# Making the high and low part of a weight unit in one operation each over 1024 columns, in two slots of a unit instead of four of a half

## The reference

```python
for l in range(2):                                   # first block
    q, k, v, u_pool, ga, gp = split(xn @ w_in[l])    # 1024 x 4096
    merged = sigmoid(ga) * (attn(q, k, v) @ w_attn_o[l]) + sigmoid(gp) * (pool(u_pool) @ w_pool_o[l])
    x = x + g1 * (merged @ w_out[l])
    x = x + g2 * peer_ffn(xf, w_query[l], sub_keys[l], expert_u[l], expert_v[l])  # all 16384 experts
# second block: half-step SwiGLU feed-forwards around neighbourhood attention (layer 0) or a short convolution (layer 1)
x = layer_norm(alpha * x + 0.5 * gate * (silu(a) * u) @ ffn_w_out, g, b)
```

## Time and profile before

| | |
|---|---|
| median of 3 runs | 4274.32 us (4267.85 to 4274.61) |
| profiled execution | span 4273.0 us, from the first to the last instruction of the program |
| TensorE matmul busy | 4056.4 us, 95% |
| VectorE busy | 2736.9 us, 64% |
| ScalarE busy | 1983.0 us, 46% |
| GpSimd busy | 105.5 us, 2% |
| mean granted TensorE clock | 0.974 of full speed |

### The profile page before, as it was taken

One profiled execution on the slowest core, in us unless ns is written; L12 is line 12 of the kernel. 1 busy time (PEld: TensorE's weight loads), 2 busy tenths in 40 slices (PEclk: granted clock), 3 DMA queues, 4 the chain that ended last, 5 costly groups with the idle time before them and its releaser, 6 DMA issues.

```text
span 4273.0 us, 85154 instructions
## 1 busy us (share of the span) xinstructions
PE 4056.4 (95%) x29544; PEld 3598.5 (84%) x29544; DVE 2736.9 (64%) x5356; ACT 1983.0 (46%) x3929; POOL 105.5 (2%) x131
## 2 busy tenths in 40 slices
PE   8999889999999999979999999989999989999998
PEld 1889245999999988824799999989999869898898
DVE  0564976666666665487666666666566665656665
ACT  0554066444444454317544444445454444444444
POOL 0000000000000000000000000001001010001010
PEclk9999989999999999989999999999999999999999
DMA  8334734555555434554455555575554315454454
GB/s 277 131 134 156 254 133 143 182 182 182 182 182 182 167 124 143 186 198 167 146 183 182 182 182 182 182 199 176 170 184 148 109 50 182 143 182 142 148 172 138
DMA packets 195899, 714.28 MB, mean 167 GB/s; under 512 B 21696, under 2 KB 22080, under 8 KB 195520
## 3 DMA queue, kind: packets, MB, share of 16 engines
q1 hardware_dynamic: 194112, 705.08, 49.5%
q0 software_dynamic: 1664, 7.57, 0.8%
HBM read 711.52 MB, written 1.05 MB: 167 GB/s over the span
## 4 chain that ended last, share of the span: by engine, by line
PE 56%; PEld 28%; DVE 10%; issue 3%; ACT 2%; PEldq 1%; DMA 1%; DVEq 0%; ACTq 0%; POOL 0%; SPq 0%; POOLq 0%
PE bank L1560 14%; PE bank L1562 14%; PE bank L1561 14%; PEld bank L1562 11%; PEld bank L1560 10%; PEld bank L1561 7%; PE bank L1676 6%; PE bank L1849 2%; PE bank L1657 2%; PE bank L1850 1%; DVE wl L898 1%; PE bank L1820 1%; PE bank L1966 1%; DVE arena L1009 0%; DVE arena L1258 0%
## 5 line engine op out<-in xcount | busy, mean ns | idle before, releaser
L898 DVE TENSOR_TENSOR wl<-raw,wh 128x512 fp32r<-128x512 f32 x2180 | 1508.3, 704 | 1082.8 <-ACT wh L520 1081.2
L520 ACT ACTIVATE wh<-raw 128x512 fp32r<-128x512 f32 x2180 | 1344.2, 629 | 1255.7 <-PE bank L1562 1251.7
L1560 PE MATMUL bank<-XH,wh 128*128 128x256 f32 x5184 | 1497.8, 289 | 97.2 <-DVE XL L1000 51.7
L1561 PE MATMUL bank<-XL,wh 128*128 128x256 f32 x5184 | 1480.9, 286 | 0.0
L1562 PE MATMUL bank<-XH,wl 128*128 128x256 f32 x5184 | 1480.4, 286 | 0.0
L1560 PEld LDWEIGHTS bank<-XH,wh 128*128 128x128 f32 x5184 | 1007.8, 194 | 118.9 <-issue 82.9
L1561 PEld LDWEIGHTS bank<-XL,wh 128*128 128x128 f32 x5184 | 1010.5, 195 | 1.1 <-issue 1.0
L1562 PEld LDWEIGHTS bank<-XH,wl 128*128 128x128 f32 x5184 | 1009.5, 195 | 0.0
L1560 PE MATMUL bank<-AH,wh 128*128 128x256 f32 x2928 | 828.7, 283 | 0.0
L1561 PE MATMUL bank<-AL,wh 128*128 128x256 f32 x2928 | 828.6, 283 | 0.0
L1562 PE MATMUL bank<-AH,wl 128*128 128x256 f32 x2928 | 828.6, 283 | 0.0
(11 more groups left out here) (223 smaller groups left out, 3251.7 us busy)
## 6 DMA issues: line engine op xcount, KB each, us to landing
raw<-stream SPq DMA_DIRECT2D x1340, 512.0 KB, 3.3
arena<-rpb POOLq DMA_DIRECT2D x4, 1024.0 KB, 24.5
arena<-tables POOLq DMA_DIRECT2D x2, 832.0 KB, 7.7
X<-x_t SPq DMA_DIRECT2D x1, 1024.0 KB, 7.8
arena<-ctx_t POOLq DMA_DIRECT2D x1, 1024.0 KB, 8.7
out_t<-X SPq DMA_DIRECT2D x4, 256.0 KB, 2.1
arena<-tables POOLq DMA_DIRECT2D x1, 608.0 KB, 14.4
cols<-columns SPq DMA_DIRECT2D x1, 218.0 KB, 2.5
```

The costliest lines, as they stand in the source:

```text
L520: act.activation(wh[:, n % 4, :], raw[:, q % 4, HALF * half:HALF * (half + 1)], ACT.Copy).then_inc(hi_ready, 1)
L898: tt_op(wl[:, n % 4, :], raw[:, q % 4, HALF * half:HALF * (half + 1)], wh[:, n % 4, :].bitcast(F32), SUB).then_inc(lo_ready, 1)
L1560: pe.matmul(out, wh[:, n % 4, a:b], moving_h, start=start, stop=False, skip_group_check=check)
L1561: pe.matmul(out, wh[:, n % 4, a:b], moving_l, start=False, stop=False, skip_group_check=check)
```

## The change

`wh` and `wl` keep their size but are divided in two slots of a whole unit. `hi` and `lo` each issue one operation over 1024 columns for a unit, where they issued two over 512. TensorE waits once for a unit and frees the slot once, after its 24th matmul; the semaphore counts units. Which matmuls run and in which order stays the same. The one-hot tiles are placed at the same addresses as before, written in the new shape. `outer` is changed in the same way as `tile`.

```diff
--- before.py
+++ after.py
@@ -207,8 +207,8 @@
     raw = sb("raw", [P, 4, UNIT])
-    wh = sb("wh", [P, 4, HALF], F32R)
-    wl = sb("wl", [P, 4, HALF], F32R)
+    wh = sb("wh", [P, 2, UNIT], F32R)
+    wl = sb("wl", [P, 2, UNIT], F32R)
...
-    SLOTS = 4
+    SLOTS = 2
...
-                    return (lo_ready, 2 * (st.s + k) + 2) if st.split else (raw_used, st.r + k + 1)
+                    return (lo_ready, st.s + k + 1) if st.split else (raw_used, st.r + k + 1)
...
         def hi(st, k, i=0, per=0):
 
             s, q = st.s + k, st.q + k
-            for half in range(2):
-                if half == 0:
-                    act.wait_ge(raw_ready[q % 4], 16 * (q // 4 + 1) + 4 * per * i)
-                n = 2 * s + half
-                act.wait_ge(halves_free, n + 1 + 2 * per * i)
-                act.activation(wh[:, n % 4, :], raw[:, q % 4, HALF * half:HALF * (half + 1)],
-                               ACT.Copy).then_inc(hi_ready, 1)
+            act.wait_ge(raw_ready[q % 4], 16 * (q // 4 + 1) + 4 * per * i)
+            act.wait_ge(slots_free, s + 1 + per * i)
+            act.activation(wh[:, s % 2, :], raw[:, q % 4, :], ACT.Copy).then_inc(hi_ready, 1)
 
         def group_done(st, k, i=0, per=0):
 
-            act.wait_ge(halves_free, SLOTS + 2 * (st.s + k + 1) + 2 * per * i)
+            act.wait_ge(slots_free, SLOTS + st.s + k + 1 + per * i)
...
         def lo(st, k, i=0, per=0):
             s, q = st.s + k, st.q + k
-            for half in range(2):
-                n = 2 * s + half
-                dve.wait_ge(hi_ready, n + 1 + 2 * per * i)
-                tt_op(wl[:, n % 4, :], raw[:, q % 4, HALF * half:HALF * (half + 1)], wh[:, n % 4, :].bitcast(F32),
-                      SUB).then_inc(lo_ready, 1)
+            dve.wait_ge(hi_ready, s + 1 + per * i)
+            tt_op(wl[:, s % 2, :], raw[:, q % 4, :], wh[:, s % 2, :].bitcast(F32), SUB).then_inc(lo_ready, 1)
...
         def tile(st, k, i, per, out, pair):
 
             awaited = st.name in made and k == 0 and per == 0
-            for half in range(2):
-                n = 2 * (st.s + k) + half
-                pe.wait_ge(lo_ready, n + 1 + 2 * per * i)
-                for kk in range(4):
-                    kt = 4 * half + kk
-                    if awaited:
-                        pe.wait_ge(xl_ready, made[st.name] - KT + kt + 1)
-                    last = three(out, n, P * kk, P * (kk + 1), pair[0][:, kt, :], pair[1][:, kt, :], kt == 0,
-                                 kt == KT - 1)
-                last.then_inc(halves_free, 1)
+            n = st.s + k
+            pe.wait_ge(lo_ready, n + 1 + per * i)
+            for kt in range(KT):
+                if awaited:
+                    pe.wait_ge(xl_ready, made[st.name] - KT + kt + 1)
+                last = three(out, n, P * kt, P * (kt + 1), pair[0][:, kt, :], pair[1][:, kt, :], kt == 0, kt == KT - 1)
+            last.then_inc(slots_free, 1)
```

More of the change, by code:

```diff
@@ L419, in _ @@
             if rounds > 0:
-                per = 8 if st.split else 4
+                per = 4
                 with sp.Fori(0, rounds) as i:
@@ L894, in lo @@
             s, q = st.s + k, st.q + k
[L895 to L899 removed]
+            dve.wait_ge(hi_ready, s + 1 + per * i)
+            tt_op(wl[:, s % 2, :], raw[:, q % 4, :], wh[:, s % 2, :].bitcast(F32), SUB).then_inc(lo_ready, 1)
         def group_done(st, k, i=0, per=0):
[L902 removed]
+            dve.wait_ge(slots_free, SLOTS + st.s + k + 1 + per * i)
         def product(st, evacuate=None, a=0, b=None, then=None):
@@ L953, in middle @@
                     k = nin + (j - 2) * per + nin
-                    dve.wait_ge(halves_free, SLOTS + 2 * (st.s + k + 1) + 2 * body * per * i)
+                    dve.wait_ge(slots_free, SLOTS + st.s + k + 1 + body * per * i)
                 dve.wait_ge(group_free, 2 + g + 1 + body * i)
@@ L1596, in outer @@
         def outer(st, k, i, per, moving_h, moving_l, first, final):
-            for half in range(2):
-                n = 2 * (st.s + k) + half
-                pe.wait_ge(lo_ready, n + 1 + 2 * per * i)
-                for kk in range(4):
-                    o = 4 * half + kk
-                    last = three(banks[o // 2][:, (o % 2) * T:(o % 2 + 1) * T], n, P * kk, P * (kk + 1), moving_h,
-                                 moving_l, first and o % 2 == 0, final and o % 2 == 1, True)
-                last.then_inc(halves_free, 1)
+            n = st.s + k
+            pe.wait_ge(lo_ready, n + 1 + per * i)
+            for o in range(KT):
+                last = three(banks[o // 2][:, (o % 2) * T:(o % 2 + 1) * T], n, P * o, P * (o + 1), moving_h, moving_l,
+                             first and o % 2 == 0, final and o % 2 == 1, True)
+            last.then_inc(slots_free, 1)
         def pairs(st, nin, hooks=None, pair=first_pair, before_acc=None):
```

14 lines of the change are left out of this document (7 added, 7 removed).

## The result

The changed kernel takes 4342.15 us, median of 4 runs (4339.29 to 4346.0), against 4273.92 us for the kernel before (4 runs, 4267.85 to 4274.61): a ratio of 1.0166, interval 1.0152 to 1.018. It is slower by 68 us.

The account below looks back on a forecast made before the run. TensorE was taken to bound the kernel, with the slots' cover falling from 2.5 to 0.13 us. Losses of 18 + 5 + 12 + 11 + 6 + 7 + 17 + 10 = 86 us on 4273.0 gave 4359 to 4360 us, range 4300 to 4425.

Parts of the forecast that it names:

- The chain: From a unit's end to TensorE's next need: copy, subtraction and hand-overs take 2.75 us against 2.88 available.
- The cover in the pairs stages: Pairs stages, 842 units: the chain still fits with 0.13 us to spare, cost 0.
- cover gone: Rival: in the pairs stages the chain takes 3.11 us, 97 us more there, 4478 us in all; chance 0.17.
- Part 2, product stages: Product stages, 208 units: ScalarE's evacuation delays the copy, 0.075 to 0.125 us a unit, 18 us.
- Part 3, w_out: w_out, 14 units: residual add and square precede the copy, chain 3.65 us, 5 us lost.
- Part 4, starts: Twelve starts of stages: TensorE waits 1.0 us for the second unit, 12 us.
- Part 5, starts under GpSimd: Three feed-forwards and conv_in: the whole unit waits behind GpSimd's operation, 11 us, plus 6 us for lower clock.
- Part 5, GpSimd's other places: The first feed-forward's start and two other places of GpSimd's L499: 7 us together.
- Part 6, pieces: Hooks making operand pieces and coefficients: the next copy comes late; three sets 14 us, other hooks 3, 17 us.
- The savings: One wide operation replacing two spares VectorE 174 and ScalarE 218 us, but gains nothing while these engines wait.
- The case that the subtraction starts first: At starts under GpSimd: GpSimd would wait instead, the 11 us shrink to 4 and the sum to 79.
- part 7: w_in's own interruptions: table loads ahead of copies and the square, 1.2 us each at 8 places, 10 us.

Follow-up runs that it names:

- the run with 0.33 us more: The changed kernel with an extra ScalarE copy of 256 columns ahead of every high part: 4436.31 us, ratio 1.0382.
- The two experiments on the order: The changed kernel with ScalarE's copy issued ahead of the evacuation in query, conv_in and w_out: 4332.73 us; the same with four whole slots: 4305.33 us.
- The split kernel: The kernel before with GpSimd's one multiplication over 128x2048 cut in eight over 128x256: 4249.4 us, ratio 0.994.
- the kernels with small updates: The changed kernel and the kernel before, each with GpSimd's updates cut to one column of each tile: 4309.52 us and 4246.51 us.

## Why the prediction was right, and the terms that were mis-sized

The forecast of 4359 us (4300 to 4425) was for slower by 86 us; it is slower by 68. Its mechanism, distance lost between a half's request and its need, held at each place where it was looked at. The sum of 86 us is 15 over the 71 of the profile. Two of its terms were too large, one group by 10 us and the four starts under GpSimd by 9; the others together come out within some 4.

- **The chain.** Release 0.20, copy 1.06, gap 0.03, subtraction 1.22 to 1.23 us: every term as predicted. The line drawn from the earlier trace rows for the copy was right to 0.01 us. The cover in the pairs stages held (5919 matmuls in 710 us). By the run with 0.33 us more it is 0.1 to 0.2 us, for 0.13 predicted. The rival "cover gone" was wrong only by this margin.
- **Part 2, product stages.** Predicted 0.075 to 0.125 us a unit; at 80 us for 645 matmuls, 24 take 2.98 us, 0.10 more than 2.88. The two experiments on the order show the place.
- **Part 3, w_out.** ScalarE's squares start at 309.05, 312.16 and 315.55: 6.50 us for two units, 0.37 over 2.88 a unit, against 0.385 predicted; the stages grew by 5.1 us, for 5 predicted.
- **Part 4, starts.** 0.67 us of visible idle, 0.83 with what the matmul row before hides, for 1.0 predicted, at the start looked at. From first matmul to the end of the fourth unit the twelve starts cost 15.5 us more than before, for 12; that holds the usual loss of product units too. One, na_o, costs nothing, the rest 0.8 to 2.6.
- **Parts 2, 4 and 7 together** were 40 us, 4 of them for kv_ctx and qkv. The rest, w_in, attn_o, pool_o, query, experts and conv_o with conv_in behind its start, grew by 26 for 36 predicted, some 10 less, twice the scatter of a profile. Which of the terms was too large no run separates.
- **Part 5, starts under GpSimd: the term whose mechanism was in part wrong.** The text said "0.7 + 12 x 0.17 = 2.7 us, at three feed-forwards and conv_in: 11", then "3 us each: 6" for the clock, 17 us for four starts. The wait itself came as forecast (over 5 us, at all four), and so did the 1.2 GHz stretch at the two starts that had kept their clock. Yet the four starts lose 70 matmuls, 8.4 us. What failed is the price per start. At the two that had kept their clock it was 2.7 + 3 us, and they lose 28 and 23 matmuls, 3.4 and 2.8 us: the low stretch was counted in full on top of 12 slow matmuls, but part of it falls into the wait, where it costs no matmuls. At the two that had lost it before it was 2.7, and they lose 5 and 14 matmuls, 0.6 and 1.7 us, since the kernel before had paid for some of the slow ones already. GpSimd's multiplication also took 4.51 us, not the 5.04 of the earlier trace rows, which brings the held subtraction's end forward by 0.5 us; why it is shorter was not tried. And little of this loss hangs on GpSimd: up to the fourth unit's end of the same starts the change costs 8.3 us with the updates whole, and 7.3 with small ones.
- **Part 5, GpSimd's other places.** 7 us were put down for three of them. The first feed-forward alone lost 1.9 at its start and 4.8 in its middle.
- **Part 6, pieces.** 17 us predicted, for three sets of 4.7 and 3 for other hooks. The set in the first feed-forward cost 5.0 us, the stage on x with its set and other hooks 6.5. The third set stands in kv_ctx.
- **kv_ctx and qkv** grew by 10.4 us. The sum had about 9 for them, 4 in part 2 and the third set of part 6, but no line of their own, and no run takes them apart.
- **The savings.** By the Trainium skill ("VectorE: DVE Perf Modes", section on the TRN2 errata), larger operands spread a fixed time per instruction. The trace agrees: 147 us less on VectorE, 192 on ScalarE, where the prediction had 174 and 218. The prediction took twice the length of a narrow row, but rows of two adjacent halves overlap (two subtractions take 1.28 us, not 1.38), so there was less to save. The time gained by it is nil, as argued from the earlier trace rows.
- **The lock.** The subtraction held behind GpSimd's operation is in the changed kernel as it was in the earlier trace rows. The Trainium skill ("SBUF — State Buffer", section "SBUF: two separate sides") calls the shared port an exclusive lock held for an operation's whole length. The split kernel agrees: at eight short operations, VectorE gets its turn between them. The case that the subtraction starts first did not come up (3571.97 against 3572.34).

What stays open: how the 13 us of the two w_in stages divide between the order, the starts and the table loads of part 7, and the same for kv_ctx and qkv. No run separated these.

## What to carry to other kernels

Where a producer chain feeds a bound engine through slots, write down two numbers before merging operations: the time from release to ready, and how long the consumer has work from the other slots. Merging halves takes from both sides, since halves let the two producing engines overlap and let the first half be handed over early; with two slots an excess is paid by half in every unit, as the product stages show (intervals of 2.87 and 3.18 us in turn). Look then at the program order of the producing engine, because an in-order wait ahead of the request sets the distance whatever the number of slots; and if a long operation of GpSimd stands beside VectorE's chain, cut it, even if GpSimd itself gets slower.

## What the runs showed of the hardware beside this

- Making the same 1024 columns in one wide copy and one wide subtraction is cheaper in busy time (1.057 and 1.225 us a unit, against 1.233 and 1.355 for two halves; the subtractions in the kernels with small updates) and 0.36 us longer from start to ready.
- A wait's length does not tell its price in clock. Behind four waits of 3.2 to 3.3 us the granted clock over 6 us was 0.50, 0.72, 1.00 and 1.00; behind four of 5.1 us, at the same starts, it was 0.65, 0.66, 0.66 and 0.75.
- Splitting GpSimd's 5.04 us operation in eight makes it 8.60 us long beside a busy VectorE, and the kernel 25 us faster. Cutting the updates to one column gives 26.
- A stall of up to some 0.16 us between matmuls shows no idle time at all (the one at 359.05 showed 0.05 us of 0.2), since rows of 0.28 us follow each other at 0.12; 61 waits of 68.8 us are therefore fewer and shorter than the stalls there were.
